# Recurrent mixer: inversion steps over all four quadrants, the transpose made from T, the directions staggered by half a level

## The reference

```python
def step(state, inp):
    r_t, w_t, k_t, v_t, kk_t, a_t = inp
    sa = jnp.einsum('bhij,bhj->bhi', state, -kk_t)
    state = (state * w_t[:, :, None, :]
             + sa[..., None] * (kk_t * a_t)[:, :, None, :]
             + v_t[..., None] * k_t[:, :, None, :])
    y_t = jnp.einsum('bhij,bhj->bhi', state, r_t)
    return state, y_t
y = (rwkv7_scan(r_h, decay[:, :, 0], ..., False)
     + rwkv7_scan(r_h, decay[:, :, 1], ..., True))
```

## Time and profile before

| | |
|---|---|
| median of 3 runs | 1899.15 us (1898.04 to 1901.95) |
| the profiled execution | 1899.53 us |
| its span | 1897.8 us |
| TensorE busy | 1823.5 us, 96% of the span |
| VectorE busy | 1092.1 us, 58% |
| ScalarE busy | 674.3 us, 36% |
| GpSimd busy | 312.7 us, 16% |
| mean granted TensorE clock | 0.988 |

### The profile page before, as it was taken

How to read it: one execution, slowest core, us unless ns; L and a number is a source line. 1 busy time by engine, 2 the same in 40 slices (tenths; PEclk the granted TensorE clock), 3 DMA queues, 4 the chain that set the end, 5 groups by cost and what they waited for, 6 DMA issues and landing times. The chain is left out here.

```text
span 1897.8 us, 36848 instructions
## 1 busy us (share of the span) xinstructions
PE 1823.5 (96%) x15870; PEld 1485.6 (78%) x15870; DVE 1092.1 (58%) x1642; ACT 674.3 (36%) x1098; POOL 312.7 (16%) x296
## 2 busy tenths in 40 slices
PE   7999999999999788999999899999999999999997
PEld 6877757688888667778888669888978888888886
DVE  4665354554257788444366887787574635354545
ACT  4334332332223577442222374433233322122342
POOL 4210011130002665310021340000001000000011
PEclk9999999999999899999999999999999999999998
DMA  5334323142223110224331100002042222322231
GB/s 191 103 108 136 137 83 133 45 189 102 90 74 111 35 38 11 73 89 140 131 102 56 49 1 4 4 3 70 4 178 92 104 104 89 111 89 89 78 100 45
DMA packets 42848, 160.87 MB, mean 85 GB/s; under 512 B 5312, under 2 KB 14528, under 8 KB 28096
## 3 DMA queue, kind: packets, MB, share of 16 engines
q1 hardware_dynamic: 28480, 143.84, 22.2%
q10 hardware_dynamic: 14208, 14.68, 2.2%
HBM read 140.42 MB, written 16.78 MB: 83 GB/s over the span
## 5 line engine op out<-in xcount | busy, mean ns | idle before, releaser
L257 DVE TENSOR_TENSOR wlo<-raw,whi 128x2048 fp32r<-128x2048 f32 (+2 forms) x113 | 251.1, 2222 | 179.0 <-ACT whi L248 178.7
L248 ACT ACTIVATE whi<-raw 128x2048 fp32r<-128x2048 f32 (+2 forms) x113 | 209.1, 1850 | 321.4 <-PE ps L283 161.3
L281 PE MATMUL ps<-act_hi,whi 128*128 128x512 f32 x616 | 243.4, 395 | 0.0
L301 PE MATMUL ps<-act_lo,whi 128*128 128x512 f32 x632 | 240.9, 390 | 0.0
L283 PE MATMUL ps<-act_hi,wlo 128*128 128x512 f32 x616 | 240.7, 391 | 0.0
L282 PE MATMUL ps<-act_lo,whi 128*128 128x512 f32 x616 | 240.4, 390 | 0.0
L300 PE MATMUL ps<-act_hi,whi 128*128 128x512 f32 x592 | 235.5, 398 | 0.0
L305 PE MATMUL ps<-act_hi,wlo 128*128 128x512 f32 x632 | 156.5, 389 | 0.0
L301 PEld LDWEIGHTS ps<-act_lo,whi 128*128 128x128 f32 x632 | 118.7, 188 | 25.3 <-issue 1.2
L305 PEld LDWEIGHTS ps<-act_hi,wlo 128*128 128x128 f32 x632 | 118.6, 188 | 24.6
L300 PEld LDWEIGHTS ps<-act_hi,whi 128*128 128x128 f32 x592 | 111.1, 188 | 32.2 <-issue 8.1
(11 more groups left out here) (552 smaller groups left out, 3478.0 us busy)
## 6 DMA issues: line engine op xcount, KB each, us to landing
raw<-stream_in SPq DMA_DIRECT2D x107, 1024.0 KB, 4.8
v_scratch<-v_out ACTq DMA_DIRECT2D x16, 256.0 KB, 3.3
z_scratch<-zt ACTq DMA_DIRECT2D x16, 256.0 KB, 3.0
mlh_v<-v_scratch SPq DMA_DIRECT2D x4, 1024.0 KB, 4.8
mlh_z<-z_scratch SPq DMA_DIRECT2D x16, 256.0 KB, 2.6
cmp_w<-cmp_w_in SPq DMA_DIRECT2D x2, 2048.0 KB, 11.3
z_scratch<-in_zt ACTq DMA_DIRECT2D x16, 256.0 KB, 3.0
mix_g<-z_scratch SPq DMA_DIRECT2D x16, 256.0 KB, 6.7
```

Of the source, the lines that this page charges most:

```text
L248: act.activation(k.whi[b % 2][:, 0:n], k.raw[b % RAW_SLOTS][:, 0:n], ACT.Copy).then_inc(k.hi_done, 1)
L257: dve.tensor_tensor(k.wlo[b % 2][:, 0:n], k.raw[b % RAW_SLOTS][:, 0:n], k.whi[b % 2][:, 0:n].bitcast(F32), ALU.subtract).then_inc(k.lo_don ...
L281: pe.matmul(bank, hi, x_hi, start=(x == 0), stop=False)
L301: pe.matmul(bank, hi, x_lo, start=False, stop=False)
```

## The change

- The steps of the inversion are written as `quarters`. The 16 products of a step are spread so that each of the four combinations of input half and output half (quadrants) gets four of them, in turn. The results of a step go to two PSUM banks, one for each input half, of which 256 columns are used; there are four such pairs of banks in turn.
- So that this fits, Z and Tt are kept in a crossed placement of heads, chunks and halves (`crossed`), and T in the old one (`straight`). `ar`, the layout of `wu`'s copies and the products around the inversion are rearranged to match (`place`, `halves_together`, `by_pair`, `by_time`). L2788 and L2833 now also use all four quadrants.
- Tt is no longer updated by a product and a masked copy. Each level's Tt is made from T by a product with the identity (step R), which ScalarE copies out (VectorE for level 0, where it also adds the identity). VectorE keeps the masked copies of T alone, ten a pair instead of eighteen; the two additions of the identity in `first_level` move behind R of level 0.
- The order of the steps is that of `steps_of`: 32 steps, direction 1 half a level behind direction 0. In pair 0 the attention's transposes are steps (A) of that list. The last level has T and R steps too.
- A step waits until the step four places before it has been copied out (before: eight places).
- The side work of VectorE and ScalarE stays at the Z steps at which it stood.

```diff
-    for lv in range(1, LEVELS):
-        ops += [("Z", lv, d) for d in range(2)]
-        for d in range(2):
-            ops += ([("T", lv, d)] if lv < final else []) + [("Tt", lv, d)]
...
+    def steps_of(c):
+
+        out = [("R", 0, 0), ("R", 0, 1), ("Z", 1, 0), ("Z", 1, 1), ("T", 1, 0)]
+        for lv in range(2, LEVELS):
+            out += [("Z", lv, 0), ("R", lv - 1, 0), ("T", lv - 1, 1)]
+            if c == 0:
+                out.append(("A", lv - 2, 0))
+            out += [("T", lv, 0), ("Z", lv, 1), ("R", lv - 1, 1)]
+        return out + [("R", final, 0), ("T", final, 1), ("R", final, 1)]
...
+    def pair_of(q):
+
+        n = 2 * (0, 2, 1, 3)[q % 4]
+        return n, k.ps[:, n:n + 2, :]
...
-    def tiles64(pe, out, lhs, x, d):
-
-        for i in range(8):
-            for par in range(2):
-                h = rows_half(par)
-                last = pe.matmul(out[h, chunk(i)], lhs[h, 8 * d + i, :], x[h, 8 * d + i, :], start=True, stop=True)
+    def straight(par, y, x):
+        return rows_half(par), 4 * (y // 2) + 2 * x + y % 2
+
+    def crossed(par, y, x):
+        return rows_half(x), 2 * y + par
+
+    def quarters(pe, name, lv, d, bank):
+
+        for y in range(4):
+            for other in range(2):
+                for source in range(2):
+                    par, x = (other, source) if name == "T" else (source, other)
+                    sh, su = straight(par, y, x)
+                    ch, cu = crossed(par, y, x)
+                    su, cu = 8 * d + su, 8 * d + cu
+                    if name == "T":
+                        to, h, lhs, y_in = sh, ch, Tt[ch, cu, :], Z[ch, cu, :]
+                    elif name == "Z":
+                        to, h, lhs, y_in = ch, sh, sc[sh, su, 0, :], T[sh, su, :]
+                    elif lv:
+                        to, h, lhs, y_in = ch, sh, T[sh, su, :], eye64[sh]
+                    else:
+                        to, h, lhs, y_in = ch, sh, eye64[sh], off[sh, su, :]
+                    last = pe.matmul(k.ps[to, bank + source, chunk(y)], lhs, y_in, start=True, stop=True)
         return last
...
-                    last = pe.matmul(k.ps[h, d, chunk(u % 8)], sc[h, u, 2, :], vtok[h, it, chunk(hd)], start=True,
-                                     stop=True)
+                    last = pe.matmul(k.ps[rows_half(it // 2), par, chunk(4 * d + 2 * hd + it % 2)], sc[h, u, 2, :],
+                                     vtok[h, it, chunk(hd)], start=True, stop=True)
...
+                order = steps_of(c)
+                for q, (name, lv, d) in enumerate(order):
                     if name == "Z":
-                        past(pe, "t", c, made["T", lv - 1, d])
+                        past(pe, "t", c, made("T", lv - 1, d))
+                    elif name == "T":
+                        past(pe, "zc", c, made("Z", lv, d))
+                        past(pe, "rt", c, made("R", lv - 1, d))
+                    elif name == "R":
+                        past(pe, "t", c, made("T", lv, d)) if lv else past(pe, "off0", c, d + 1)
+                    if q == 1:
+                        past(pe, "t", c, 2)
+                    elif q in (2, 3) and c + 1 < RW_T:
+                        past(pe, "sigs", c + 1, 2 * q - 2)
+                    elif q >= 4:
+                        held, at, side = order[q - 4]
+                        if held == "A":
+                            pe.wait_ge(daa["y_lo"], at + 1)
+                        else:
+                            past(pe, {"Z": "zc", "T": "t", "R": "rt"}[held], c, made(held, at, side))
...
+                for d in range(2):
+                    past(pe, "rt", c, made("R", final, d))
+                    for y in range(4):
+                        for par in range(2):
+                            for x in range(2):
+                                h, u = crossed(par, y, x)
+                                last = pe.matmul(k.ps[rows_half(par), 2 * d + x, chunk2(y)], Tt[h, 8 * d + u, :],
+                                                 rhs[h, 8 * d + u, :], start=True, stop=True)
+                                if y == 3 and par == 1:
+                                    last.then_inc(ss["wum"], 1)
...
+                    if name == "R" and lv:
+                        past(act, "rz", c, made(name, lv, d))
+                        act.activation(by_pair(Tt, d), from_pair(two), ACT.Copy).then_inc(ss["rt"], 1)
                     if name == "Z":
-                        past(act, "z", c, made[name, lv, d] + 2)
+                        past(act, "z", c, made(name, lv, d) + 2)
                         if lv > 1:
-                            past(act, "tz", c, made["Tt", lv - 1, d] - 4)
-                        act.activation(units(Z, d).rearrange("p u t -> p (u t)"), bank_of(op), ACT.Copy) \
-                            .then_inc(ss["zc"], 1)
+                            past(act, "tz", c, made("Z", lv - 1, d))
+                        act.activation(by_pair(Z, d), from_pair(two), ACT.Copy).then_inc(ss["zc"], 1)
...
-                past(dve, "off0", c, d + 1)
-                dve.tensor_tensor(units(Tt, d), units(off, d), eye, ALU.add).then_inc(ss["t"], 1)
...
+                    if name == "R" and lv == 0:
+                        past(dve, "rz", c, made(name, lv, d))
+                        dve.tensor_tensor(by_pair(Tt, d), from_pair(two), eye, ALU.add).then_inc(ss["rt"], 1)
...
-                    n += 1
-                    past(dve, "tz", c, n)
-                    x = T if name == "T" else Tt
-                    past(dve, "t", c, made[name, lv - 1, d])
-                    dve.copy_predicated(units(x, d), level_mask(lv, d if name == "Tt" else 1 - d).bitcast(U32),
-                                        bank_of(op).rearrange("p (u t) -> p u t", t=CHUNK)).then_inc(ss["t"], 1)
+                    if name == "T":
+                        past(dve, "tz", c, made("Z", lv, d))
+                        past(dve, "t", c, made("T", lv - 1, d))
+                        dve.copy_predicated(by_time(T, d), level_mask(lv, 1 - d).bitcast(U32),
+                                            two[:, :, 0:256].rearrange("p a (h m) -> p a h m", h=2)).then_inc(ss["t"], 1)
```

More of the change, by code:

```diff
@@ L2667, in stage_rw_heads, with by_pair, by_time, from_pair @@
     eye = eye64.rearrange("p (o n) -> p o n", o=1).to_broadcast([P, 8, CHUNK])
-    def bank_of(op):
-        return k.ps[:, op % 8, :]
     def units(x, d):
         return x[:, 8 * d:8 * d + 8, :]
+    def by_pair(x, d):
+        return x[:, 8 * d:8 * d + 8, :].rearrange("p (y a) n -> p a y n", a=2)
+    def by_time(x, d):
+        return x[:, 8 * d:8 * d + 8, :].rearrange("p (h a y) n -> p a h (y n)", h=2, a=2)
+    def from_pair(two, d=0):
+        return two[:, :, 256 * d:256 * d + 256].rearrange("p a (y n) -> p a y n", y=4)
     def chunk(t):
         return slice(t * CHUNK, (t + 1) * CHUNK)
+    def place(t):
+        return chunk(2 * (t % 4) + t // 4)
     def r_of(c):
@@ L2831, in _ @@
+                places = [(d, hd, it, 8 * d + 4 * hd + it) for d in range(2) for hd in range(2) for it in range(TT)]
+                for d, hd, it, u in places:
+                    if hd == it == 0:
+                        past(pe, "wu_a", c, d + 1)
+                        past(pe, "wu_d", c, d + 1)
                     for par in range(2):
                         h = rows_half(par)
-                        last = pe.matmul(k.ps[h, u // 4, chunk2(u % 4)], Tt[h, u, :], rhs[h, u, :], start=True, stop=True)
@@ L2834, in _ @@
[L2834 to L2839, removed]
-                    for par in range(2):
-                        h = rows_half(par)
-                        last = pe.matmul(k.ps[rows_half(hd), 4 + par, chunk(4 * d + it)], wu[h, u, 0:64], sc[h, u, 1, :],
+                        last = pe.matmul(k.ps[rows_half(hd), 4 + par, chunk(4 * d + 2 * (it % 2) + it // 2)], wu[h, u, 0:64], sc[h, u, 1, :],
@@ L2891, in _ @@
                                 h = rows_half(hd)
-                                last = pe.matmul(k.ps[rows_half(par), 4 + hd, chunk(it)], ar[c % 2][h, d, 1, chunk(t)],
+                                last = pe.matmul(k.ps[rows_half(par), 4 + hd, chunk(it)], ar[c % 2][h, d, 1, place(t)],
                                                  state[h, d, t, :], start=(d == 0), stop=(d == 1))
@@ L2945, in _ @@
                                 x()
-                for g in (0, 2):
-                    past(act, "wum", c, g + 1)
-                    act.activation(wu[:, 4 * g:4 * g + 4, :].rearrange("p u t -> p (u t)"), k.ps[:, g, :], ACT.Copy) \
+                for d in range(2):
+                    past(act, "wum", c, 2 * d + 1)
+                    act.activation(by_time(wu, d)[:, 0], k.ps[:, 2 * d, :].rearrange("p (h m) -> p h m", h=2), ACT.Copy) \
                         .then_inc(ss["wu_a"], 1)
@@ L3099, in _ @@
                         .then_inc(ss["t"], 1)
-                n = 0
-                for op, (name, lv, d) in enumerate(ops):
```

(15 more changed lines are left out.)

87 lines of the change are left out of this document (36 added, 51 removed).

## The result

| | before | after |
|---|---|---|
| median of the runs, us | 1898.65 | 1925.56 (1920.4 to 1929.1) |
| ratio, 95% interval | 1 | 1.0136 (1.0110 to 1.0162) |
| span of the profiled execution, us | 1897.8 | 1924.1 |
| mean granted clock | 0.988 | 0.974 |
| first step to first state step, pairs 0 to 3, us | 44.6, 40.6, 40.5, 40.2 | 48.9, 52.2, 47.4, 47.0 |

The change costs 27 us. The sign was forecast, the size was not: 1904.4 in a range of 1893 to 1918.

A forecast was written before the change was run, and what follows sets the result against it. It took the chain of steps and the side work to set the inversions: 1899.5 + 3.9 (inversions to state steps) - 3.7 (L2788) + 5.1 (clock) = 1904.8, less 0.4 for the median: 1904.4 us, range 1893 to 1918.

The forecast's parts named there:

- The rate of a step: Inversion steps: 32 records on four quadrants occupy TensorE for 0.49 us, result after 0.74, from L2892's 15 ns a record.
- Rival (d): Inversion steps: four quadrants don't keep 15 ns a record, a step stays at 0.80 us; 1923 us, chance 0.09.
- The layout of the waits: Pair 1's inversion: first masked copy of T at 7.3 us, TensorE standing still from 3.0 to 8.1.
- TensorE then has 32 x 0.49 = 15.7 us of work: Inversion of a pair: 32 steps at 0.49 us each, so TensorE no longer hides the other engines.
- From the last R copy to the first state step: After each inversion: `wu` at half its 3.48 us, the state step 11.9 us after the last R copy.
- The clock term: Inversion steps slowed by falls of TensorE's clock after gaps without matmuls, together +5.1 us.
- The clock in the inversions, +5.1 us: Clock falls after gaps: 2.0 us in each of pairs 1 and 2, 0.4 and 0.7 in pairs 0 and 3.
- Rival (c): Inversions of pairs 1 and 2: the clock stays low through both, 16 us, giving 1915 us; chance 0.10.

The follow-up runs named there:

- the faster kernel: The changed kernel with side work in pieces, R steps of levels 1 to 5 as transposes and a wide product before each: 1888.9 us (0.9955).
- the last experiment: Idle matmuls put into TensorE's gaps, against the changed kernel with R steps as transposes (1910.8 us): 1915.0 us (1.0086).

## Why the prediction was wrong

By its own steps:

- **The rate of a step: right.** 0.47 us for 32 records in a row and 0.69 to the result after a wait (1210.26, 1212.61), against 0.49 and 0.74. `L2788`'s product takes 1.21 in place of 2.08. Rival (d) had a time near the result (1923) and the wrong mechanism, and the 25 ns of the Trainium skill ("TensorE: Matmul & The Clock Gate", "Wait — 56ns, not 53.3ns?") fall with it: records of four quadrants are 15 ns apart over whole steps.
- **The layout of the waits: right.** First masked copy at 7.3 us (1217.58), as laid out; level 2's Z at 8.1, as laid out; the wait for ScalarE's R copy in level 4 is there, 2.4, 2.4 and 1.4 us in pairs 0 to 2. From level 3 on the order still held and the times didn't: Z of levels 3, 4 and 5 at 13.5, 19.1 and 25.9 us, laid out at 11.7, 15.3 and 21.4. In front of level 2 TensorE stood 5.0 us in pair 1 and 3.5 in pair 2, where a stop had come first. Shortening these waits gave 18.5 us, most of it VectorE's.
- **The step that failed: "TensorE then has 32 x 0.49 = 15.7 us of work".** It took the rate of `L2892`, 1 us and 128 instructions long, as what TensorE can keep, and asked only whether the quadrants keep it. They do, and the instruction stream does not. 15.7 us of work are 2048 instructions, eight blocks of 256, each used up in 1.9 us; where TensorE had a stop at both ends of a block, the block took 3.85, which makes 31 us for the eight (an estimate), however fast the steps are. By the same count the 28 steps of before are seven blocks and 27 us, and they took 26.5: the kernel before already ran at about the pace of its instructions, and the change added a block. From the first step to the last R copy I had 30.3, 32.7, 32.7 and 27.6 us (123.3); measured were 34.7, 38.6, 33.7 and 34.3 (141.3), 18.0 more, of which 5.1 were booked under the clock. 16.6 us of stops lie there. They are not all on the chain, so the sizes don't simply add. A quarter fewer instructions gave 14.8 and 15.3 us, and slower steps were free until the stops were gone.
- **The trace of before could have told.** Its fetches 3.6 to 4.1 us apart are one sign; its timeline of TensorE also has pauses of this kind in `L2857`, which uses four quadrants, in pairs 0 and 1:

```profile
1178.07 0.27 PE L2857 MATMUL ps<-rw_vtok,rw_tok 64*64 64x64 f32 x1 [0.32 <-issue]
...
1241.18 0.30 PE L2857 MATMUL ps<-rw_vtok,rw_tok 64*64 64x64 f32 x4 [0.38 <-issue]
```

  Both end 2.6 us after a fetch began. I had seen them and taken them for noise. The question to ask was what 256 instructions take at the new rate, against how far apart the fetches are.
- **From the last R copy to the first state step:** 11.9 forecast; 14.2, 13.6, 13.7 and 12.7 measured, 6.5 in all. The mechanism was right, and `wu` was mis-sized: at 2.4 GHz it takes the 1.7 us of the forecast (1.71 in four pairs of the faster kernel, where the stretch is 11.4 to 12.0), but in the changed kernel it ran mostly at 1.2 GHz and took 3.0 to 3.2, nearly the 3.4 of before. The clock term had looked at the steps alone.
- **The clock in the inversions, +5.1 us: right in pair 1, not priced as a whole.** In pair 1 it fell to 1.2 GHz from 1217.4 to 1224.2, after the 5 us without a matmul, and with no stop yet the third level's Z came 1.8 us later than laid out, against the 2.0 allowed. Over all four inversions the only price is the 2.7 us of the last experiment, net of its idle matmuls, and in another kernel. Rival (c) had the clock low through both inversions and 16 us; it was low for 13.4 and 6.8 us in them. That the 33 us at the lower level lie beside waits or take the place of stops is argued, not shown.
- **What is left** of the 21 us: 18.0 + 6.5 less the 5.1, 1.1 us by which the stage began later, with 27.3 us at the lower clock in the stages ahead of it in place of 20.5, which the change does not touch, and 0.5 in the products between the inversions, where TensorE has 2.0 us under "issue".

On the mechanism the Trainium skill, "Runtime: NRT & Kernel Launch", "Instruction fetch mechanics", has half of it: instructions come in blocks of 16 KiB, 256 of them, fetched ahead by a DMA queue of the engine's own. By the 130 packets of 2.13 MB the trace agrees. It adds that this is mostly hidden, because instructions are issued more slowly than they are filled in. Here that holds at 3.7 us a block, with a pause of 0.3 in the inversions of before, and fails at 1.9.

## What to carry to other kernels

Before a product is made faster by using more of the array, count its instructions: what one block of 256 takes at the new rate, against the 3.4 us at least, 3.85 in the median, that a block took here with a stop at both ends. Beyond that point fewer instructions per result (transposes instead of products with the identity, wider moving operands) pay and faster ones don't. And where one engine's steps were the cover for two others' side work, halve the steps only together with cutting that side work into pieces.

## What the runs showed of the hardware

- TensorE's instruction stream gave it 256 matmuls and weight loads in 3.4 us at the least and 3.85 in the median (46 blocks, eight kernels): idle times of 0.1 to 1.7 us inside a step, whole blocks of 256 apart (90 of 90), ended 2.1 to 2.9 us after a fetch of 16 KB began. At 14 to 15 ns a record (7 ns an instruction, 1.9 us a block) this is what bounds; at 29 ns (3.7 us a block) TensorE ran nearly without a stop.
- The records of small float32 products on four quadrants start 15 ns apart for as long as instructions last (32 in 0.47 us), and on two 29 ns apart (0.93).
- Low clock and short supply can hide each other: with the clock held at 0.96 to 1.00, the inversions were 139.1 us in place of 137.4.
- The waits view puts two things under "issue": a stop for instructions, and a wait for ScalarE's copy where the T step waits for two semaphores. Only the length and the place inside or ahead of a step tell them apart.
